# Filler products around the transposes and sums of four attention stages

## The reference

```python
# first block, in each of two layers: 6 heads, one key and one value head shared
logits = einsum('bqhd,bqkd->bqhk', qj, kg) * HEAD_DIM ** -0.5   # 64 selected keys
p = softmax(logits);  out = einsum('bqhk,bqkd->bqhd', p, vg)
# second block, layer 0: 16 heads with a forget term
s = q k^T * scale + c_i - c_j, causal;  p = softmax(s);  out = p v
# second block, layer 1: per group of 8 heads three attentions, gated and added
o = g0 * (compressed, 15 keys) + g1 * (selected) + g2 * (window)
```

## Time and profile before

| | us |
|---|---|
| median of three runs | 2462.19 |
| lowest, highest | 2450.63, 2462.84 |
| the profiled execution | 2450.4 |
| its span from first to last instruction | 2448.6 |
| PE busy | 2318.8 |
| DVE busy | 1841.5 |
| ACT busy | 1328.3 |

### The profile page before, as it was taken

One profiled execution on the slowest core, in us unless ns is written; L12 is line 12 of the kernel. 1 busy time (PEld: TensorE's weight loads), 2 busy tenths in 40 slices (PEclk: granted clock), 3 DMA queues, 4 the chain that ended last, 5 costly groups with the idle time before them and its releaser, 6 DMA issues.

```text
span 2448.6 us, 30711 instructions
## 1 busy us (share of the span) xinstructions
PE 2318.8 (95%) x12633; PEld 1909.2 (78%) x12633; DVE 1841.5 (75%) x2233; ACT 1328.3 (54%) x1333; POOL 34.2 (1%) x62
## 2 busy tenths in 40 slices
PE   7989999988899999999999999997889999888999
PEld 4766999657688888888888888875778997656998
DVE  4756564676788989898989898985747887765887
ACT  4333443443477777777777777763444433465432
POOL 1000000000000000000000000000000000000000
PEclk9988999997999999999999999998979999879999
DMA  9635655571599999999999999992415554402553
GB/s 341 230 128 172 216 189 189 199 272 44 169 376 350 365 350 364 352 363 352 362 353 362 353 362 353 362 346 90 159 34 178 184 184 143 138 1 83 187 189 104
DMA packets 281283, 584.44 MB, mean 239 GB/s; under 512 B 12030, under 2 KB 86892, under 8 KB 281008
## 3 DMA queue, kind: packets, MB, share of 16 engines
q1 hardware_dynamic: 277600, 572.33, 66.3%
q0 software_dynamic: 3536, 10.08, 1.3%
HBM read 581.32 MB, written 1.05 MB: 238 GB/s over the span
## 4 chain that ended last, share of the span: by engine, by line
PE 86%; DVE 7%; ACT 4%; DMA 2%; issue 1%; POOL 0%; DVEq 0%; ACTq 0%; POOLq 0%
PE ps L1270 24%; PE ps L1271 24%; PE ps L1272 24%; PE ps L1323 2%; DMA raw<-in_w_ada 1%; PE ps L1402 1%; PE ps L1387 1%; DVE w_lo L1894 1%; PE ps L1654 1%; ACT arena L984 1%; PE ps L1514 1%; DVE arena L1911 1%; PE ps L1425 1%; PE ps L1671 1%; DVE arena L2116 1%
## 5 line engine op out<-in xcount | busy, mean ns | idle before, releaser
L888 ACT ACTIVATE w_hi<-raw 128x2048 fp32r<-128x2048 f32 x500 | 948.5, 1906 | 426.3 <-PE ps L1272 320.7
L1894 DVE TENSOR_TENSOR w_lo<-raw,w_hi 128x2048 fp32r<-128x2048 f32 x500 | 1116.9, 2271 | 31.1 <-ACT w_hi L888 28.7
L1270 PE MATMUL ps<-w_hi,xT_hi 128*128 128x512 f32 (+1 forms) x1408 | 552.7, 393 | 16.0 <-DVE w_lo L1894 7.3
L1271 PE MATMUL ps<-w_lo,xT_hi 128*128 128x512 f32 (+1 forms) x1408 | 546.2, 388 | 0.0
L1272 PE MATMUL ps<-w_hi,xT_lo 128*128 128x512 f32 (+1 forms) x1408 | 546.0, 388 | 0.0
L1270 PEld LDWEIGHTS ps<-w_hi,xT_hi 128*128 128x128 f32 x1408 | 269.9, 192 | 70.2 <-DVE w_lo L1894 7.3
L1272 PEld LDWEIGHTS ps<-w_hi,xT_lo 128*128 128x128 f32 x1408 | 269.7, 192 | 53.8
L1271 PEld LDWEIGHTS ps<-w_lo,xT_hi 128*128 128x128 f32 x1408 | 269.9, 192 | 50.6
L1270 PE MATMUL ps<-xT_hi,w_hi 128*128 128x256 f32 x1056 | 299.7, 284 | 3.7 <-DVE xT_lo L1945 3.7
L1271 PE MATMUL ps<-xT_lo,w_hi 128*128 128x256 f32 x1056 | 299.6, 284 | 0.0
L1272 PE MATMUL ps<-xT_hi,w_lo 128*128 128x256 f32 x1056 | 299.5, 284 | 0.0
(11 more groups left out here) (360 smaller groups left out, 2040.1 us busy)
## 6 DMA issues: line engine op xcount, KB each, us to landing
raw<-in_moe_w_gate SPq DMA_DIRECT2D x112, 1024.0 KB, 5.5
raw<-in_moe_w_up SPq DMA_DIRECT2D x112, 1024.0 KB, 5.3
raw<-in_moe_w_down SPq DMA_DIRECT2D x112, 1024.0 KB, 5.6
raw<-in_w_ada SPq DMA_DIRECT2D x48, 1024.0 KB, 5.8
raw<-in_f_w_up SPq DMA_DIRECT2D x44, 1024.0 KB, 5.1
raw<-in_f_w_down SPq DMA_DIRECT2D x22, 1024.0 KB, 5.0
raw<-in_w_in SPq DMA_DIRECT2D x20, 1024.0 KB, 7.4
raw<-in_a_w_in SPq DMA_DIRECT2D x12, 1024.0 KB, 5.2
```

The costliest lines, as they stand in the source:

```text
L888: act.activation(w_hi[:, k % HI, 0:size], raw[:, r, 0:size], ACT.Copy).then_inc(ring.w_hi_ready, 1)
L1270: pe.matmul(out_, lh, rh, start=start, stop=False)
L1271: pe.matmul(out_, lh, rl, start=False, stop=False)
L1894: dve.tensor_tensor(w_lo[:, k % RAW, 0:size], raw[:, k % RAW, 0:size], w_hi[:, k % HI, 0:size].bitcast(F32), ALU.subtract).then_inc(ring.w ...
```

## The change

PE's `attend` gets a function `busy(i)`, called twice in each step whose sums are of a part that isn't "heads": ahead of the transposes, and again between scores and sums. For a part that is first, last or only it issues two float32 products of 128 x 128 by 128 x 256 (identity and constants) into the bank of 2 and 3 that holds no running sum, behind a wait for `att_taken`, so that what was in the bank has been taken. For the middle part of three it does nothing. Nothing reads what it writes. No other engine's instructions change.

```diff
+                def busy(i):
+                    o = at.outs(i) - at.last[i]
+                    if not at.first[i] and not at.last[i]:
+                        return
+                    free = 2 + (o if at.first[i] else o + 1) % 2
+                    done = o - 1 if at.first[i] else o
+                    if done > 0:
+                        pe.wait_ge(att_taken, done)
+                    for _ in range(2):
+                        pe.matmul(ps[:, free, 0:256], ident, const[:, 0:256], start=True, stop=True)
...
                 for k in range(n + 4):
+                    summed = 0 <= k - 4 < n and at.parts[k - 4][0] != "heads"
+                    if summed:
+                        busy(k - 4)
                     if at.lead <= k - 3 < n:
                         transposed(k - 3)
                     if k < n and at.parts[k][0] != "heads":
                         scores(k)
-                    if 0 <= k - 4 < n and at.parts[k - 4][0] != "heads":
+                    if summed:
+                        busy(k - 4)
                         sums(k - 4)
```

## The result

The changed kernel is slower by 0.3%: 1.003 of the time of before, with a 95% interval of 1.0017 to 1.0042. Its median over 15 runs is 2462.98 us (2457.35 to 2471.64), that of before 2454.16 us over as many (from 2450.41 up). By the ratio that is some 7.4 us, by the two medians 8.8. The first three runs of before had given a median of 2462.19. One of the fifteen runs of before, of 2923.96 us, fell in a slow state and isn't compared.

What follows compares the result with a forecast made beforehand. PE, 95% busy, bounds the kernel, slowed by low clock and gaps in four attention stages. Stage terms of +4.1, +5.6, +2.5 and +3.3 make +15.5, less 3.5 gives +12 on the median 2462.2: 2474 us, range 2450 to 2494.

Steps and rivals of the forecast that it cites:

- the 22.4 us of waits for ACT's copies: PE's gaps at the transposes: 2.5, 2.7, 3.4 and 13.8 us in the four stages, all set against the fillers.
- The sum over the stages: Forecast lengthening of the two dsa stages, fa and nsa: fillers and added wait less waits covered and clock gain, +15.5 us.
- the fillers: 64 calls in the four stages at 0.87 us, 55.7 us, plus 1.75 us a stage for two calls at low clock.
- PE's other work, by the clock: Low-clock PE work behind the first calls halves: -3.3 and -1.5 in dsa, -3.0 and -6.8 in fa, -1.5 and -11.0 in nsa.
- PE's idle time: Four stages: waits covered, -2.5, -2.7, -3.4 and -13.8 us, against 1.1 us of added wait in each dsa stage.
- added wait: Third dsa step's filler waits for output 0, +1.1 us a stage; as rival at most 6.6 us, 2478, chance 0.13 with other mixes.
- The allowance for the luck of the profile of before: 3.5 us taken off the sum: an average execution before should have more low-clock time in nsa for fillers to save.
- the shift of the base: Whole kernel: the difference laid on the three-run median, 11.8 us above the profiled execution's 2450.4.
- The clock that doesn't rise: Rival, four stages: level stays as before despite fillers; +66 us, 2528; chance 0.12, including a rise in part.
- The full payment: Rival, four stages: level rises with the first call, all 80.05 us halved, waits covered; -13, 2449 us; chance 0.20.
- half of the clock's rival: Level rises in only part of the stretches in the four stages: about +35 us, 2497; range end named after it, 2494.
- The estimate from the Trainium skill: Low-clock stretches: half the whole throttled 94 us counted as its cost, so gain at most 47 us, not 40.

Runs made afterwards that it cites:

- second pair: The kernel before and the changed kernel, each profiled once more unchanged: stages together 185.04 and 193.32 us, single runs 2454.95 and 2460.48 us.
- fillers at the waits: Against the kernel before: two-product calls mainly where PE waits in the four attention stages, and `turns` ahead of nsa lengthened from 9 to 12 products; ratio 0.9945, again 0.9950.
- the run without products: The changed kernel with `busy` keeping its two waits but issuing no product; 2454.66 us, ratio 1.0013 to before.

## Why the prediction was right or wrong

**The direction and the mechanism were right.** The level rises after two calls in the first stage, at about 142.4 us, holds 0.99 to 1.00 from about the third filler to the end of each stage, and of the 22.4 us of waits for ACT's copies 0.9 are left. What the change loses is the time of its products beyond that.

**The sum over the stages came out near the first pair of profiles by errors that cancel, and by luck.** It had +4.1, +5.6, +2.5 and +3.3, together +15.5; the first pair of profiles has +4.0, +5.3, +1.2 and +4.1, together +14.6. Term by term, in us over the four stages (the fillers are read from start to start, the rest from PE's busy and idle time; the second pair is that of the second profiles):

| term | the sum | first pair | second pair | fillers at the waits, against the first profile of before |
|---|---|---|---|---|
| the fillers | +62.7 | +68.4 | +65.6 | +39.3 |
| PE's other work, by the clock | -27.1 | -32.0 | -31.4 | -34.7 |
| PE's idle time | -20.2 | -21.7 | -25.9 | -17.8 |
| together | +15.4 | +14.6 | +8.3 | -13.3 |

A call at the high clock took 0.98 us in the mean and not 0.87: I halved the time of a record of 512 columns. The clock gave back 4 to 5 us more than I counted, and the waits 1.5 to 5.7. Of the added wait, 1.1 us in each dsa stage, the run without products shows 0.73 in the first one. That these errors leave +15.4 beside +14.6 is luck, for the first pair sets the fastest of fifteen executions of before against the second slowest of fifteen of the changed kernel. The second pair, nearer to the medians, has +8.3. The last column shows the cause from the other side: with 29 us less of filler the clock gives back as much, and the stages get shorter.

**What failed is the step from the profiled execution to the time.** 2474.0 was 11.0 us too high, though 2462.98 lies in the range. 8.0 of the 11.0 are the base: I laid the difference on the median of three runs, 2462.19, which was itself a draw, for over 15 runs before has 2454.16. Read against that median the prediction forecast a slowdown of 0.8%, where 0.3% was measured.

The other 3 us are the size of the change, +12 where the medians have 8.8 and the ratio 7.4. The allowance for the luck of the profile of before, 3.5 us, was about right: its profile stands 3.8 us under the median, and in the second profile its stages are 3.6 longer. It is the changed kernel that I put too high. The sum makes its stages 181.48 + 15.4 = 196.9 us, and the second profile, nearer to the median, has 193.3. The figure without the shift of the base, 2462.4, would have met the measured median, but by luck: its base is 3.8 us too low and its change 3 too high.

**The rivals.** The clock that doesn't rise did not come in the changed kernel, but it is real: with fillers of a quarter of the array two stages stayed at 0.53 and 0.57. I had set it aside by what the products are; these runs fit that in the dsa stages, and in fa up to the late rise, and not in nsa. The full payment did not come with two places either; the waits in nsa were all used, and the fillers there still cost more than the clock and the waits gave. The added wait alone is about 3 us, half of what its rival had, with an interval from -0.5 to 6.6 that doesn't shut it out. The range ended at 2494 us, where half of the clock's rival, after which I named that end, comes to 2497; nothing hangs on it. The estimate from the Trainium skill (47 us as the ceiling in place of 40, "TensorE: Matmul & The Clock Gate", "HAM oscillation — how this bites in real kernels") isn't tested here: the fillers fill the gaps in the same runs in which the level rises, so no run shows what the clock alone does to them.

**What I said of the two places** holds: the first covers waits, and a delay made in the second is in part made good at the next wait (7.1 us left of 13.8 in nsa). 0.9991 and 1.0006 alone, 1.003 together: the second place added to the first costs 0.39%, 9.6 us, for the 31 us that its 32 calls take.

What stays open: why nsa kept its level with the small fillers and the dsa stages did not; how much of the gain of the fillers at the waits is that of the longer `turns`; and how far the 2.5 us more of nsa with the waits alone are the wait's.

## What to carry to other kernels

A product that nobody reads costs nothing where PE waits anyhow. Elsewhere it costs its time, and has to bring back more by the clock. Here 64 calls made the kernel 0.3% slower, and some 36, put at the waits as far as possible (with a longer `turns` ahead of nsa), made it 0.5% faster; in nsa, once the waits were used up, each further pair of products cost 0.89 to 0.96 us. Find the stretches at the low clock and the wait ahead of each, and size the filler to that wait. Where two executions of one kernel differ by more than the effect, count a stage's gain from two profiles at least, and don't lay a sum from one profile on a median of three runs: here that median was 8 us off.

## What the runs showed of the hardware

A float32 product of 128 x 128 by 128 x 256 took two records of 0.24 us each at the high clock where two of them stood in a row, and of 0.228 where eight did (16 records in 3.65 us, four products a call). One by 128 x 512 took two of 0.435. In the first dsa stage PE busy for 28.54 of 31.07 us kept 1.2 GHz nearly throughout, where the same number of records with fillers on the whole array had the level up after two calls. In fa, with the same small fillers, the level stayed at 0.50 through 21 us of PE without a gap and only then rose. In the first recurrence the 10 us behind a wait of 3.17 us ran at 0.70, and at 1.00 with that wait filled.
